# One program per engine for output projection and feed-forward of a mixed attention and state-space layer

## What is computed

```python
x = x + jnp.concatenate([o_nsa, ssm_glu(y_ssm, p)], axis=-1) @ p['w_out']
...
def ffn_block(x, hist, p):
    hu = rmsnorm(x, p['norm_ffn']) @ p['w_up']
    hp = jnp.concatenate([hist.astype(hu.dtype), hu], axis=1)
    c = lax.conv_general_dilated(hp, p['conv_w'][:, None, :], ...) + p['conv_b']
    a, g = jnp.split(c, 2, axis=-1)
    return x + (jax.nn.silu(a) * g) @ p['w_down'], hp[:, -(CONV_W - 1):]
```

## Time and profile before

| | us |
|---|---|
| median of three runs | 1994.75 (1992.07 to 1998.62) |
| the profiled execution | 1998.57 |
| its span in the trace | 1996.9 |
| PE busy | 1787.3 (90%) |
| DVE busy | 915.0 (46%) |
| ACT busy | 567.9 (28%) |
| POOL busy | 307.6 (15%) |

### The profile page before, as it was taken

How to read it: one execution, slowest core, us unless ns; L and a number is a source line. 1 busy time by engine, 2 the same in 40 slices (tenths; PEclk the granted TensorE clock), 3 DMA queues, 4 the chain that set the end, 5 groups by cost and what they waited for, 6 DMA issues and landing times. The chain is left out here.

```text
span 1996.9 us, 27094 instructions
## 1 busy us (share of the span) xinstructions
PE 1787.3 (90%) x10875; PEld 1502.0 (75%) x10876; DVE 915.0 (46%) x1404; ACT 567.9 (28%) x876; POOL 307.6 (15%) x265
## 2 busy tenths in 40 slices
PE   5999788856998999886869979999999999999988
PEld 4655778854555554545649979999999999999977
DVE  3456004673544443417121055555555555555554
ACT  4000013553443343320221133232222222222222
POOL 0000000022212211210011012222222222222210
PEclk8999897977999999896989979999999999999999
DMA  6312414401333322536010021112111111211102
GB/s 257 65 43 107 157 49 153 164 39 53 96 95 112 121 85 86 197 134 199 4 63 22 1 75 40 55 32 63 32 60 35 34 61 32 63 32 57 37 11 90
DMA packets 94796, 155.15 MB, mean 78 GB/s; under 512 B 19670, under 2 KB 72446, under 8 KB 92366
## 3 DMA queue, kind: packets, MB, share of 16 engines
q1 hardware_dynamic: 81200, 93.82, 14.7%
q0 software_dynamic: 12672, 58.73, 8.8%
q10 hardware_dynamic: 848, 1.54, 0.3%
HBM read 133.61 MB, written 24.83 MB: 79 GB/s over the span
## 5 line engine op out<-in xcount | busy, mean ns | idle before, releaser
L2224 PE MATMUL ps<-h_up,w_split 128*128 128x344 f32 x2112 | 403.5, 323 | 9.2 <-DVE h_rest L2394 7.4
L2403 DVE TENSOR_TENSOR xT<-ps,xT 128x1032 f32<-128x1032 f32 x176 | 216.9, 1233 | 316.8 <-PE ps L2224 316.8
L2224 PEld LDWEIGHTS ps<-h_up,w_split 128*128 128x128 f32 x2112 | 344.1, 189 | 20.1 <-issue 16.5
L2224 PE MATMUL ps<-gated,wd_split 128*128 128x344 f32 x1584 | 266.8, 324 | 3.0 <-POOL wd_split L2380 2.1
L2224 PEld LDWEIGHTS ps<-gated,wd_split 128*128 128x128 f32 x1584 | 250.5, 188 | 12.7 <-DVE xT L2403 7.8
L2224 PE MATMUL ps<-h_rest,w_split 128*128 128x344 f32 x1056 | 225.0, 321 | 0.0
L2224 PEld LDWEIGHTS ps<-h_rest,w_split 128*128 128x128 f32 x1056 | 179.5, 190 | 0.0
L2410 DVE SCALAR_TENSOR_TENSOR cv<-hu,ccol,cv 128x1024 f32<-128x1024 f32 x88 | 142.7, 1622 | 16.4 <-ACT cv L2322 10.7
L2320 ACT ACTIVATE hu<-ps 128x1032 f32<-128x1032 f32 x44 | 45.4, 1033 | 331.9 <-PE ps L2224 331.9
L2360 POOL TENSOR_TENSOR w_split<-w_raw,w_split 128x1024 fp32r<-128x1024 f32 x44 | 107.0, 2433 | 188.1 <-ACT w_split L2305 188.1
L1601 DVE TENSOR_REDUCE top<-ps 128x1 f32<-128x384 f32 (+4 forms) x124 | 71.3, 586 | 139.4 <-PE ps L1226 73.6
(11 more groups left out here) (436 smaller groups left out, 2514.1 us busy)
## 6 DMA issues: line engine op xcount, KB each, us to landing
w_raw<-in_w_up SPq DMA_DIRECT2D x44, 512.0 KB, 6.1
wd_raw<-in_w_down SPq DMA_DIRECT2D x22, 512.0 KB, 3.6
unit<-in_cache_kv_win POOLq DMA_DIRECT2D x16, 512.0 KB, 4.6
x_kept<-xT SPq DMA_DIRECT2D x1, 4128.0 KB, 25.4
xT<-x_kept SPq DMA_DIRECT2D x1, 4128.0 KB, 19.6
xtok<-in_x_prompt SPq DMA_DIRECT2D x2, 2048.0 KB, 8.1
w_qu<-in_w_in SPq DMA_DIRECT2D x2, 2048.0 KB, 8.6
w_out_sb<-in_w_out SPq DMA_DIRECT2D x4, 1024.0 KB, 5.0
```

Source lines behind the costliest of these rows:

```text
L2224: mm = pe.matmul(k.ps[:, bank + c, 0:TG], w(wn), x(xn)[:, c * TG:c * TG + TG], start=start and m == 0, stop=stop and m == 2)
L2403: dve.tensor_tensor(x, k.ps[:, bank:bank + 3, 0:TG], x, ALU.add).then_inc(added, 1)
```

## The change

The two stages become one block, so the border between them goes. In each engine's program:

- **PE**: of the eight sums over squares two are left, both behind the last products: one over a total of blocks 0 to 6, one over block 7. Half of the history's transposes (22) stand ahead of `multiply`, half behind it.
- **POOL** adds the squares of blocks 0 to 6 into `sq_total` (six adds, from block 4 on), and makes the rest of the two first `w_raw` tiles among them.
- **ACT** issues two of the three DMAs at the start of the output projection, and splits the two first `w_raw` tiles behind the squares of blocks 2 and 3.
- **SP** issues the four quarters of `w_out` and both `w_raw` tiles one behind the other with no wait (a semaphore for each quarter now), then waits for the last product and issues `hist_row`.
- The tensors move: `mix_up` is cut in `mix_low` and `mix_high`, and `w_out_sb` makes room for `w_raw`.

```diff
+class PooledMean(Mean):
+    def square(self, k, act, sq, d):
+        if d >= 2:
+            act.wait_ge(self.pooled, max(1, d - 2))
+        act.activation(sq[:, d % 2], k.xT[:, d], ACT.Square, scale=D_MODEL ** -0.5).then_inc(self.squared, 1)
+    def pool(self, pool, sq, total, d):
+        pool.wait_ge(self.squared, d + 1)
+        if d >= 2:
+            pool.wait_ge(self.pooled, d - 1)
+        pool.tensor_tensor(total[:], sq[:, 0] if d == 1 else total[:], sq[:, d % 2], ALU.add).then_inc(self.pooled, 1)
+    def sum(self, k, pe, sq, total, m):
+        if m == 0:
+            pe.wait_ge(self.pooled, KD - 2)
+        else:
+            pe.wait_ge(self.squared, KD)
+        x = (total[:], sq[:, (KD - 1) % 2])[m]
...
-            for q in range(4):
-                sp.dma_start(k.w_out_sb[:, :, 2 * P * q:2 * P * (q + 1)],
-                             ...).then_inc(w_in, 16)
-                sp.wait_ge(w_in, 16 * (q + 1))
+        for q in range(4):
+            sp.dma_start(k.w_out_sb[:, :, 2 * P * q:2 * P * (q + 1)],
+                         ...).then_inc(self.w_in[q], 16)
...
                 mm.then_inc(product, 1)
-                if d:
-                    mean.sum(k, pe, k.sq_ffn, d - 1)
-            mean.sum(k, pe, k.sq_ffn, KD - 1)
+        self.mean.sum(k, pe, k.sq_ffn, k.sq_total, 0)
+        self.mean.sum(k, pe, k.sq_ffn, k.sq_total, 1)
...
+            act.wait_ge(self.added, d + 1)
+            self.mean.square(k, act, k.sq_ffn, d)
+            if d in (2, 3):
+                first_weights(d - 2)
...
+    def gpsimd(self, pool, first_rest):
+        for d in range(KD):
+            pool.wait_ge(self.w_upper, d + 1)
+            pool.tensor_tensor(k.wo_split[:, d % 2, 1], self.columns(d), ..., ALU.subtract).then_inc(self.w_rest, 1)
+            if d >= 4:
+                self.mean.pool(pool, k.sq_ffn, k.sq_total, d - 3)
+            if d in (4, 5):
+                first_rest(d - 4)
+        for d in (5, 6):
+            self.mean.pool(pool, k.sq_ffn, k.sq_total, d)
...
+            w_out.sync(sp)
             load_up(0, 0, a_in)
             load_up(0, 1, g_in)
+            sp.wait_ge(w_out.product, KD)
+            sp.dma_start(k.hist_row[:], k.dram["state_ffn_conv"][0].rearrange("b r n -> (b r) n")).then_inc(hist_in, 16)
             load_down(0)
...
+            w_out.tensor(pe)
+            pe.wait_ge(hist_in, 16)
+            turn_history(0)
+            pe.wait_ge(w_out.mean.rooted, 1)
             scaling.multiply(pe)
-            pe.wait_ge(hist_in, 16)
-            for f in range(2 * NF): ...
+            turn_history(1)
```

More of the change, by code:

```diff
@@ L252, in root, with __init__, gather @@
         act.wait_ge(self.inverted, done)
-        act.activation(k.stat[:, 3], k.stat[:, 2], ACT.Sqrt)
+        return act.activation(k.stat[:, 3], k.stat[:, 2], ACT.Sqrt)
+class PooledMean(Mean):
+    def __init__(self, nc, tag):
+        super().__init__(nc, tag)
+        self.pooled = nc.alloc_semaphore(f"pooled_{tag}")
+        self.rooted = nc.alloc_semaphore(f"rooted_{tag}")
+    def square(self, k, act, sq, d):
[13 more added lines that the diff above has]
+        x = (total[:], sq[:, (KD - 1) % 2])[m]
+        for t in range(NT + 1):
+            n = P if t < NT else NB
+            mm = pe.matmul(k.ps[0:n, 3, 2 * t + m:2 * t + m + 1], x[:, t * P:t * P + n], k.ones[:, 0:1], start=True, stop=True)
+        mm.then_inc(self.summed, 1)
+    def gather(self, k, dve):
+        dve.wait_ge(self.summed, 2)
+        dve.tensor_reduce(k.stat[:, 0, 0:NT], k.ps[:, 3, 0:2 * NT].rearrange("p (t d) -> p t d", d=2), AX.X, ALU.add)
+        dve.tensor_reduce(k.stat[0:NB, 0, NT:NT + 1], k.ps[0:NB, 3, 2 * NT:2 * NT + 2], AX.X, ALU.add).then_inc(self.inverted, 1)
+        dve.wait_ge(self.inverted, 1)
+        self.invert(k, dve, 1)
+    def root(self, k, act, done=2):
+        super().root(k, act, done).then_inc(self.rooted, 1)
 class Scaling:
@@ L2023, in _, with plan_w_out @@
                                          ALU.add, ALU.mult).then_inc(glu_out, 1)
-def stage_w_out(nc, k):
+def plan_w_out(nc, k):
     at = k.at
     k.mix_rest, _ = at("mix_rest", [P, KD, TOK], F32R, k.off_mix)
-    k.mix_up, o = at("mix_up", [P, KD, TOK], F32R, k.off_u)
-    k.w_out_sb, o = at("w_out_sb", [P, KD, D_MODEL], F32, o)
-    k.wo_split, o = at("wo_split", [P, 2, 2, KD, P], F32R, o)
[L2033 to L2047, removed]
-            for q in range(4):
-                sp.dma_start(k.w_out_sb[:, :, 2 * P * q:2 * P * (q + 1)],
-                             k.dram["w_out"][0].rearrange("(a p) n -> p a n", p=P)[:, :, 2 * P * q:2 * P * (q + 1)]).then_inc(w_in, 16)
-                sp.wait_ge(w_in, 16 * (q + 1))
[L2053 to L2067, removed]
-                if d:
-                    mean.sum(k, pe, k.sq_ffn, d - 1)
-            mean.sum(k, pe, k.sq_ffn, KD - 1)
[L2072 to L2079, removed]
-            for a in range(KD):
[L2081 to L2108, removed]
@@ L2166, in stage_ffn @@
     scaling = Scaling(nc, k, "ffn", 8, k.off_factor)
+    w_out = WOut(nc, k)
     mean = Mean(nc, "final")
@@ L2212, in _, with turn_history @@
         def _(pe):
[L2213 to L2218 removed]
+            def turn_history(z):
+                for f in range(z * NF, (z + 1) * NF):
+                    mm = pe.transpose(k.ps[:, 7 - 4 * z, f % NF * 16:f % NF * 16 + 16], k.hist_row[:, f * P:f * P + P],
+                                      k.ident[0:2 * NB, 0:2 * NB])
+                mm.then_inc(turned, 1)
+            w_out.tensor(pe)
+            pe.wait_ge(hist_in, 16)
+            turn_history(0)
+            pe.wait_ge(w_out.mean.rooted, 1)
+            scaling.multiply(pe)
+            turn_history(1)
             def product(bank, w, x, start, stop):
@@ L2298, in _ @@
         def _(act):
-            act.dma_start(k.hist_row[:], k.dram["state_ffn_conv"][0].rearrange("b r n -> (b r) n")).then_inc(hist_in, 16)
             act.dma_start(k.dram["s_ffn_conv"][0, :, 0], k.dram["state_ffn_conv"][0, :, 1]).then_inc(hist_out, 16)
@@ L2305, in upper @@
                 act.activation(k.w_split[:, z, 0], k.w_raw[:, z], ACT.Copy).then_inc(w_upper, 1)
+            w_out.scalar(act, lambda z: upper(0, z, (a_in, g_in)[z]))
             scaling.keep(act)
-            upper(0, 0, a_in)
-            upper(0, 1, g_in)
             for a in range(KD):
@@ L2365, in note, with first_rest @@
                                  k.hu[:, z, SEQ:TOK + 2]).then_inc(noted, 1)
-            for z in range(2):
+            def first_rest(z):
                 pool.wait_ge(w_upper, z + 1)
                 rest(z)
+            w_out.gpsimd(pool, first_rest)
             def body(f, first, last):
@@ L2384, in _ @@
         def _(dve):
+            w_out.vector(dve)
             dve.sem_inc(added, 8)
```

81 lines of the change are left out of this document (73 added, 8 removed).

## The result

The change is faster: 1979.72 us (median of 4 runs, 1976.03 to 1981.82) against 1996.68 us for the kernel before, ratio 0.9914, 95% interval 0.9887 to 0.9941. A second series gave 0.9910 (0.9891 to 0.9929). The profiled execution took 1981.82 us, its span is 1980.1 us (before 1998.57 and 1996.9).

A forecast was written before the change was run, and what follows sets the result against it. PE's own instructions were taken to bound the output projection, with a wait for weights in the stretch behind it. The terms -12.4 + 2.8 - 4.4 = -14.0 us, taken from the median 1994.75, gave 1980.8 us, range 1974 to 1986.5.

The forecast's parts named there:

- the likeliest case: Whole kernel: the forecast itself, 1980.8 us, faster by over 0.3%, given a chance of 0.68.
- Six sums, 12.4 us won: Output projection blocks: six sums over squares leave PE, each 2.06 us of its time, 12.4 us won.
- the adds on POOL cost nothing: Output projection: POOL's longest load per block, 9.7 us, stays under 11.29 us, so its adds cost nothing.
- The start, 2.8 us lost: Start of the output projection: ACT's two early transfers delay the first `w_out` quarter, 2.8 us lost, bounds 0 to 4.3.
- The rival of a quarter that lands last: Start: the first `w_out` quarter shares time with all loads and lands 30 us late; 2008 us, chance 0.05.
- The join, 4.4 us won: Last output projection add to first up product: early weight splits shorten 22.86 us to A+18.45 (A: that add), 4.4 us won.
- `hist_row`'s landing: Ahead of the first transposes: the unknown, taken as 6.8 us after issue at the last product; 3.6 us the alternative.
- the 18 to 19 that were named as the sign of being right: Last add to first up product: 18 to 19 us there would show the forecast right.
- the sign that the prediction named, a wait of PE for this DMA: Ahead of the transposes: the DMA of `hist_row` would be what ends PE's wait.
- The best case of 6.75 us: Last add to first up product: with `hist_row` landing in 3.6 us, 6.75 us won instead of 4.4.
- The estimate from the Trainium skill's page: Landing of `hist_row`: an estimated 5.5 us from port rate plus fixed cost, 1.3 us better, left out of the sum.
- The quicker join, as a rival: Last add to first up product: `hist_row` lands early and `multiply` runs at full clock; 1976.3 us, chance 0.20.

The follow-up runs named there:

- experiment 1: The change with the sums over squares back on PE, one behind each block's products, and no squares added on POOL: 1994.08 us, 0.9979 of the kernel before.
- (8): The change with each of POOL's six adds followed by a second operation of the same size: 1979.43 us in one execution.
- 9: The change with each of POOL's six adds followed by three more operations of the same size: 1996.93 us in one execution.
- (7): The change with ACT's two transfers (history copy, `gain_row`) issued behind the square of block 2 instead of at the start: 1981.10 us in one execution.
- experiment 6: The change with `hist_row` issued behind the first `w_down` tile and the next two `w_raw` tiles, instead of ahead: 1983.15 us in one execution.
- Experiments 3: The change with ACT's splits of the first two `w_raw` tiles behind `keep` and POOL's rests behind its adds, loads still early: 1985.08 us in one execution.
- experiment 4: The change with only POOL's rests of the first two `w_raw` tiles put back behind `keep`, ACT's splits still early: 1981.56 us in one execution.

## Why the prediction was right

1980.8 us was forecast, 1979.72 came; faster by over 0.3%, as the likeliest case had it. The mechanism held: the sums gone from a PE without a gap carry most of it, the join the rest. By its steps:

- **Six sums, 12.4 us won: right** in size (12.19) and cause (experiment 1: 12.0). That the adds on POOL cost nothing is shown up to twice the work (8), and that lateness there would stand on PE's path by 9.
- **The start, 2.8 us lost: the term was too large**, 1.0 us at the first matmul and 0.56 at the first add. Taking ACT's share of the bytes from the border's transfers was the wrong step: the quarter, issued ahead of both, landed 1.0 us later beside them and not 2.8. ACT's two transfers are the cause (7). The rival of a quarter that lands last is out; its premise of six loads in flight did not come about either, as SP issued the `w_raw` loads only behind the quarter's landing.
- **The join, 4.4 us won: too small a term**, 5.82 measured. What was named as the unknown decided it: `hist_row`'s landing, taken at 6.8 us from a row with five transfers beside it, was 5.1 us and no longer bound (4.9 to 5.2 in all kernels but before and experiment 6). The 1.4 us between forecast and measured join are the start of the transposes, 5.38 us behind the last add instead of 6.8; the 17.04 us lie below the 18 to 19 that were named as the sign of being right. With that, the sign that the prediction named, a wait of PE for this DMA, is absent from the profile of the change; experiment 6 brings it out. The best case of 6.75 us was missed because the last sum ran at a falling clock and took 1 us more. With the sums between the blocks it had taken 2.07 us, before and in experiment 1, so taking them away goes with a cost here that the prediction did not have; why is open. The estimate from the Trainium skill's page "SBUF — State Buffer", 5.5 us, was nearer to the 5.1 us measured than the row was; its 104 GB/s stand in the section "Door 1: The DMA port swizzle", its 2 us in "The DMA setup-cost knee".
- **Why a late split costs so much was only half seen.** The prediction counted ACT's waits for the weights and one `h_rest` beside POOL. Experiments 3 and 4 show that with the loads early the wait goes and the loss stays, as POOL's rests now meet DVE's scales: each of DVE's operations that meets a rest waits for a whole one. What wins is that POOL's rests have left the join.
- **The quicker join, as a rival:** its first half came, its second did not; `multiply` ran at 0.50 (4.30 us).

The two terms that were off both lay on the cautious side, 2.2 and 1.4 us; against the span's -16.8 the forecast was -14.0. The median of the kernel before in later series (1996.68 to 1997.41) lies 2 to 3 us above the 1994.75 from which the forecast was taken. That the time came within 1.1 us is luck: the win was taken 3 us too small and the start of the sum 2 us too low, and the two nearly cancel.

## What to carry to other kernels

Move work off the engine that is busy without a gap, and ask of the engine that takes it not only whether it has time but whom it blocks there: the same POOL operation was free beside PE's products and cost 2.2 us apiece beside a DVE operation with two inputs in SBUF. In a stretch with little work, look for instructions that an engine takes in order ahead of the one that everybody waits for; 22 transposes stood 1.3 us in the way of `multiply` with a free place behind it. When a change to one stretch is worth under 3 us here, read the stretch in the trace, since the time of the whole does not resolve it.

## What the runs showed of the hardware that was not expected

- DVE and POOL took turns instruction by instruction: 3.48 and 3.37 us for scales of 1.25 us (experiment 4).
- The granted clock fell in the join whether PE had gaps or not (0.75, then 0.50 with the gaps filled). Between long products a sum of the same kind had left it at 1.00.
- At the start the clock rises at nearly the same moment in both profiles (0.50 from 1044 to 1046, then 0.95 before and 0.97 in the change from 1046 to 1048), though PE began at 1041.78 before and at 1042.75 in the change: an engine that starts 1 us later was only 0.5 us later at the first add.
- From the first up product to the end, fourteen profiled executions took 827.2 to 831.8 us. The loop is either 742.9 to 743.3 or 744.5 to 744.7 us long, and the stretch from the loop's last step to the last stage either 50.7 to 50.8 or 53.0 to 53.6 us, in combinations that do not follow the edits.
